# Moving the PEER score copies of token tiles 2 to 4 from VectorE to ScalarE in a diffusion backbone step

## The chip, the cores and the metric

The kernel runs on one core of one Trainium2 chip. The metric is the device time of one execution in microseconds. Three executions of the kernel before took 2545.37, 2546.10 and 2546.45 us, so the median is 2546.1 us.

## What is computed

One layer of a backbone with two token streams: 128 context tokens and 512 latent tokens, width 1024, all in f32. The tokens are cut into five tiles of 128: tile 0 is the context, tiles 1 to 4 are the latent. Each tile goes through adaLN, a gated linear recurrence, grouped-query attention, an output projection, and then through PEER, a product-key mixture of very many small experts:

```python
q = (xb @ w_q).reshape(n, P_HEADS, 2, P_QDIM // 2)
s = jnp.einsum('nhpd,hpkd->nhpk', q, sub_keys)        # 8 heads x 2 halves x 128 keys
s1, i1 = lax.top_k(s[:, :, 0], P_TOPK); s2, i2 = lax.top_k(s[:, :, 1], P_TOPK)
...                                                   # best 16 of the sums of pairs
u = jnp.take(w_u, idx, axis=0)                        # 16384 rows of 1024
act = gelu(jnp.einsum('nhkd,nd->nhk', u, xb))
v = jnp.take(w_v, idx, axis=0)
return jnp.einsum('nhk,nhkd->nd', g * act, v)
```

Every token reads 8 x 16 = 128 expert rows (u and v side by side, 8 KB).

## The kernel before

**Slots.** A slot is one expert of each of the 128 tokens of a tile: GpSimd (POOL) gathers 128 rows of 8 KB from HBM with an indirect DMA, VectorE takes the dot of the u half with the token (`dot_of`, line 1400), ScalarE applies Gelu and the routing weight (`w_slot`, lines 945 and 951), and the v half is added to an accumulator: by VectorE (`v_row`, line 1428), or by TensorE as a product with a diagonal matrix that ScalarE writes (line 961). A tile has 128 slots, five tiles have 640. VectorE also routes (lines 1320 to 1377: top 16, indices, softmax weights), 16 slots at a time.

**The plan.** Slots 0 to 191 are woven into the dense part of the layer. `plan_groups` writes down the order of all PSUM results (`NAMES`) and, by a cost of each result on TensorE (`STAGES`), the result behind which each slot stands (`SLOT_AT`). Every engine walks the same order; its `Beside` object runs the slots that are due before it turns to a result (`beside.before(name)`, inside `start` on TensorE and `group` on VectorE and ScalarE). For tile 1's first 64 slots (128 to 191) even slots are accumulated by `v_row`, odd slots by `v_odd` (line 570, matmuls at line 577), which TensorE does two slots later (`PE_LAG`). GpSimd gathers these slots one behind another (`gather_odd`, line 1223) into six buffers; one is free again when `v_row` or `v_odd` of its slot is done.

**Dense work around the change.** `post(b)` does the output projection, the second norm and the PEER scores for a batch of tiles; batch 2 is tiles 2, 3 and 4. Its last part is 16 rounds. In round m TensorE projects the queries (`qp`: 16 matmul records of 128x384) and, behind the next projection, multiplies them with the keys (`ss`: 6 matmul records of 128x128). Its order is qp 0, qp 1, ss 0, qp 2, ss 1, ... qp 15, ss 14, ss 15. ScalarE copies each qp result out of PSUM (line 1138), VectorE copies each ss result out in three pieces, one for each tile (line 1732). qp and ss results alternate over four PSUM banks, so that a qp has the bank of the qp before the last, and an ss that of the ss before the last.

**Behind the rounds.** The remaining 448 slots (64 of tile 1, 128 of each of tiles 2 to 4) run in loops without dense work. Their gathers go round eight buffers, three of them the ring that holds the weight slabs of the rounds, so GpSimd waits for the last ss result first (line 1280). VectorE reads the copied scores of tiles 2 to 4 only there. From tile 1's slot 192 on TensorE does all the accumulating (line 590). A tile ends with its gate and final norm (`tile_end`).

`step(...)` (lines 436 to 447) makes an engine wait for its own instruction before the next.

Of the kernel before, what the change touches and what calls it, by code (L numbers as in the profile page):

```python
# [32 lines left out]
ACT = mybir.ActivationFunctionType  # L33
AX = mybir.AxisListType.X

P = 128
# [10 lines left out]
PH, TOPK, NKEYS = 8, 16, 128  # L47
# [65 lines left out]
def turn_order(tiles):  # L113

    order = []
    for i in range(len(tiles) + 1):
        order.extend([("x2T", tiles[i])] if i < len(tiles) else [])
        order.extend([("h2", tiles[i - 1])] if i else [])
    return order
# [125 lines left out]
def build(nc, x_prompt, x_sample, cols, rows, normf_rows, brow, consts, masks, sel, cond_rows, ada_slabs, col_slabs, in_slabs, o_slabs,  # L245
          out_slabs, pq_slabs, uv, state, ckT, cv, y_prompt, y_sample, new_state, new_k, new_v):
    with ExitStack() as ctx:
# [3 lines left out]
        def sem(name):  # L251
            return ctx.enter_context(nc.semaphore(name))
# [108 lines left out]
        SC = [R1[:, 0:2048], HG[:, 2048:4096], R1[:, 0:2048], AB[:, 10240:12288], AB[:, 1024:3072]]  # L361
# [9 lines left out]
        def h_tile(t, k):  # L371
            return hTp[:, k, :] if t == 0 else hTl[:, k, (t - 1) * P:t * P]
# [44 lines left out]
        qkT_ready, sm_ready, p_ready, pT_ready, ob_ready = (sem("qkT_ready"), sem("sm_ready"), sem("p_ready"),  # L417
                                                            sem("pT_ready"), sem("ob_ready"))
        pn_ready, oT_ready, sig2_ready, m_ready = sem("pn_ready"), sem("oT_ready"), sem("sig2_ready"), sem("m_ready")
        h2T_ready, h2T_half, h2_ready, qp_ready = sem("h2T_ready"), sem("h2T_half"), sem("h2_ready"), sem("qp_ready")  # L420
        kv_out, state_out, y_out, nf_in, zb_ready = (sem("kv_out"), sem("state_out"), sem("y_out"), sem("nf_in"),
                                                     sem("zb_ready"))

# [49 lines left out]
        def wait_full(eng, name):  # L473

            banks, _, count = PLACE[name]
            eng.wait_ge(full[banks[0]], count)
            return psum(name)

        def freed(name):
            return [free[b] for b in PLACE[name][0]]  # L480
# [452 lines left out]
        def _(act):  # L933
            step = Steps(act, act_step)
            A = nc.scalar.activation
# [32 lines left out]
            def group(name):  # L968

                beside.before(name)  # L970
                return wait_full(act, name)
# [44 lines left out]
            for wc, dst, fn, ready in WT:  # L1016
                for m in range(4):
                    ps = group(("winP", wc, m))
# [90 lines left out]
            def tile_root(t):  # L1109
                act.wait_ge(fss_ready, t + 1)  # L1110
                A(st[:, 30:31], st[:, 29:30], ACT.Sqrt).then_inc(frt_ready, 1)

            def post(b):
                tiles, N = BATCHES[b], NB[b]
                lo, hi = tiles[0], tiles[-1] + 1
                beside.before(("x2T", lo))
                act.wait_ge(ssq_ready, NT + hi)
                step(A(st[:, 16 + lo:16 + hi], st[:, 8 + lo:8 + hi], ACT.Sqrt), *[rms_ready] * len(tiles))
                act.wait_ge(am_ready, 3)
                for name, t in turn_order(tiles):  # L1120
                    ps = group((name, t))
                    if name == "x2T":
                        for k in range(KD // 2):
                            step(A(h_tile(t, k), ps[:, k * P:(k + 1) * P], ACT.Identity,
                                   scale=AM[:, 1, min(t, 1), k:k + 1], bias=ADA[:, 2, min(t, 1), k:k + 1]))
                        act.sem_inc(freed((name, t))[0], 1)
                        act.sem_inc(h2T_ready, 1)
                    else:
                        if t == 0:
                            act.wait_ge(state_out, 32)  # L1130
                        step(A(H2[t], ps, ACT.Copy), *freed(("h2", t)), h2_ready)
                if b == 1:
                    tile_root(0)
                for m in range(2 * PH):
                    ps = group(("qp", b, m))
                    if m >= 2:
                        wait_full(act, ("ss", b, m - 2))
                    step(A(QP[b][:, m % 2, :], ps[:, 0:N], ACT.Copy), *freed(("qp", b, m)), qp_ready)
                    if b == 1 and m == 6:
                        expos(PH)  # L1140

# [11 lines left out]
            for wc, dst, fn, ready in WT:  # L1153
                for m in range(4):
                    ps = group(("winT", wc, m))
# [145 lines left out]
        def _(dve):  # L1301
            step = Steps(dve, dve_step)
# [131 lines left out]
            def group(name):  # L1434

                beside.before(name)
                return wait_full(dve, name)
# [59 lines left out]
            for n in range(NFIRST):  # L1497
                row(n + 1)
                s, q = ADA_SEGS[n // 4], n % 4
                ps = group(("mod", n))  # L1500
# [16 lines left out]
            for n in range(NFIRST + 1, NADA):  # L1517
                col_dots(next(cols))
                row(n)
                t = n - XT_FROM  # L1520
# [175 lines left out]
            def post(b):  # L1696
                tiles, N = BATCHES[b], NB[b]
                if b == 0:
                    dve.wait_ge(gate_ready, 8)
                else:  # L1700
                    dve.wait_ge(xr_in, 64)
                for q in range(4):
                    for t in tiles:
                        cs = slice(q * SC_W, (q + 1) * SC_W)
                        ps = group(("y", q, t))
                        gate = (G1P if t == 0 else G1L)[:, cs]
                        step(V.tensor_tensor(SQ2[b][:, 0:SC_W], ps[:, 0:SC_W], gate, ALU.mult), *freed(("y", q, t)))
                        step(V.tensor_tensor(X1[t][:, cs], X1[t][:, cs], SQ2[b][:, 0:SC_W], ALU.add))
                        if q == 3:
                            ssq(X1[t], t, SQ2[b])  # L1710
                beside.before(("x2T", tiles[0]))
                for t in tiles[:2]:
                    normed(NT + t, X1[t], xn2(t))
                for i, t in enumerate(tiles):
                    if i > 1:
                        beside.before(("x2T", t))
                        normed(NT + t, X1[t], xn2(t))
                    ps = group(("x2T", t))
                    for k in range(KD // 2, KD):
                        step(V.tensor_scalar(h_tile(t, k), ps[:, k * P:(k + 1) * P], AM[:, 1, min(t, 1), k:k + 1],  # L1720
                                             ADA[:, 2, min(t, 1), k:k + 1], ALU.mult, ALU.add))
                    dve.sem_inc(freed(("x2T", t))[1], 1)
                    dve.sem_inc(h2T_half, 1)
                if b == 1:
                    tile_end(0)
                    step(V.memset(PL[:, :], 0.0))
                    dve.sem_inc(v_done, NPE)
                for m in range(2 * PH):
                    ps = group(("ss", b, m))
                    ms = slice(m * NKEYS, (m + 1) * NKEYS)  # L1730
                    for i, t in enumerate(tiles):
                        step(V.tensor_copy(SC[t][:, ms], ps[:, i * P:(i + 1) * P]))
                    for x in freed(("ss", b, m)):
                        dve.sem_inc(x, 1)
                    if b == 1 and 1 <= m <= 6:
                        route(PH, 2 * m - 2, 2 * m)
                    if b == 1 and 7 <= m < 7 + EARLY // 2:
                        route(PH + 1, 2 * m - 14, 2 * m - 12)
# [54 lines left out]
            post(2)  # L1793
            beside.rest()
            dve.wait_ge(h2_ready, NT)
            for t in range(1, NT):
                def pass_(p, last):
                    for h in range(2):
                        j = t * PH + p * 2 + h
                        nxt = early = None  # L1800
                        if not last:
                            nxt = route_parts(j + 1, 1 - h, SC[t], 0)
                            early = route_parts(j + 2, h, SC[t], (p * 2 + h + 2) * 2 * NKEYS)
                        else:
                            if not h or t + 1 < NT:
                                nxt = route_parts(j + 1, 1 - h, SC[t], 0)
                            if t + 1 < NT:
                                early = route_parts(j + 2, h, SC[t + 1], h * 2 * NKEYS)
                        for k in range(TOPK):
                            i = h * TOPK + k  # L1810
                            dot(j * TOPK + k, k, h, GB_, gb_in,
                                16 * ((t * TSLOT - NSLOT) // NGB) + p * (16 * HSLOTS // NGB) + 16 * (i // NGB + 1), H2[t])
                            ahead = early if ROUTE_AT.get(k, EARLY) < EARLY else nxt
                            if k in ROUTE_AT and ahead:
                                ahead(ROUTE_AT[k])

                if t == 1:
                    pass_(2, False)
                else:
                    with dve.Fori(0, 3) as p:  # L1820
                        pass_(p, False)
                pass_(3, True)
                tile_end(t)
# [81 lines left out]
```

## Time and profile before

| what | value |
|---|---|
| median of the three runs | 2546.1 us |
| the profiled execution | 2541.14 us, of which its span is 2539.3 us |
| mean granted TensorE clock | 0.929 |
| busy: TensorE, VectorE, ScalarE, GpSimd | 79%, 69%, 37%, 37% |
| moved by DMA | 805.53 MB, 317 GB/s over the span |
| the 16 rounds of tiles 2 to 4 | about 1256 to 1383 us of the span |
| the loops behind them | from 1383.9 us to the end |

Busy time says how long an engine executed, not whether anybody waited for it; for that the timeline of each engine and the list of waits are read, stretch by stretch.

### The profile page before, as it was taken

How to read it: one execution, taken by the hardware profiler on the slowest of the kernel's cores; microseconds unless marked ns; L12 is line 12 of the kernel's file. 1: busy time of each engine (PE TensorE's matmuls, PEld its weight loads, DVE VectorE, ACT ScalarE, POOL GpSimd, SP SyncE). 2: the span in 40 equal slices, each digit the busy share in tenths (PEclk: the TensorE clock that was granted, in tenths of full speed). 3: DMA queues.
4: the chain of work that ended last, by engine and by line, in shares of the span. 5: the costliest groups of instructions: out<-in, count | busy, mean ns of one | idle time of the engine just before them, and what ended most of it. 6: DMA issues, size and time to landing. Idle time of an engine off the chain costs nothing. (4 is left out here: it accounts for less than half of the span.)

```text
span 2539.3 us, 27322 instructions
## 1 busy us (share of the span) xinstructions
PE 2006.7 (79%) x6925; PEld 1101.4 (43%) x6925; DVE 1748.4 (69%) x3969; ACT 945.2 (37%) x2456; POOL 938.2 (37%) x774
## 2 busy tenths in 40 slices
PE   6978897966677798778698776887778887687876
PEld 2667844755566543366454222322223222232222
DVE  2732277886776678767787777777777777777764
ACT  1402144223343434312332444444444444344443
POOL 0020022232222122202233554656545666456654
PEclk9998998987888899889899998999999999999999
DMA  8844677851111498859798999999999999999997
GB/s 318 291 150 170 227 297 294 328 209 67 67 67 67 159 339 328 325 217 402 271 367 323 422 421 393 419 422 422 421 400 412 422 422 421 410 406 422 422 421 327
DMA packets 113299, 805.53 MB, mean 317 GB/s; under 512 B 12596, under 2 KB 14006, under 8 KB 17046
## 3 DMA queue, kind: packets, MB, share of 16 engines
q0 software_dynamic: 93760, 680.96, 66.7%
q1 hardware_dynamic: 17704, 118.17, 12.6%
q10 hardware_dynamic: 1712, 4.98, 0.5%
q8 instruction: 50, 0.82, 0.1%
q14 instruction: 73, 0.60, 0.1%
HBM read 800.79 MB, written 3.28 MB: 317 GB/s over the span
## 5 line engine op out<-in xcount | busy, mean ns | idle before, releaser
L1201 POOL DMA_INDIRECT RG<-in_uv,idxs x264 | 351.2, 1330 | 568.0 <-DVE pl L1428 328.0
L945 ACT ACTIVATE agel<-apre 128x1 f32<-128x1 f32 x640 | 129.2, 202 | 990.3 <-DVE apre L1400 987.2
L590 PE MATMUL pl<-RG,BP 128*128 128x512 f32 x576 | 294.0, 636 | 106.7 <-ACT BP L961 106.0
L590 PE MATMUL pl<-RING,BP 128*128 128x512 f32 x576 | 282.2, 621 | 62.2 <-ACT BP L961 60.8
L615 PE MATMUL pa<-HL,RING 128*128 128x512 f32 (+2 forms) x960 | 315.5, 487 | 8.5 <-DVEq L447 8.1
L1400 DVE CUSTOM_DVE_ANT_0 R<-RG,AB 128x1024 f32<-128x1024 f32 x201 | 246.7, 1230 | 101.9 <-DMA RG<-in_uv,idxs 81.9
L1201 POOL DMA_INDIRECT RING<-in_uv,idxs x168 | 253.3, 1508 | 155.7 <-PE pl L590 68.6
L1400 DVE CUSTOM_DVE_ANT_0 R<-RING,AB 128x1024 f32<-128x1024 f32 x168 | 205.9, 1226 | 95.0 <-DMA RING<-in_uv,idxs 78.1
L615 PEld LDWEIGHTS pa<-HL,RING 128*128 128x128 f32 x960 | 166.3, 196 | 149.8 <-issue 119.1
L590 PEld LDWEIGHTS pl<-RG,BP 128*128 128x128 f32 x576 | 99.8, 192 | 294.0 <-ACT BP L961 220.1
L961 ACT ACTIVATE BP<-CT,wexp 128x128 f32<-128x128 f32 x480 | 192.7, 401 | 53.4 <-PE pl L590 15.9
L590 PEld LDWEIGHTS pl<-RING,BP 128*128 128x128 f32 x576 | 104.1, 194 | 235.6 <-ACT BP L961 145.6
L951 ACT ACTIVATE wexp<-agel,gws 128x1 f32<-128x1 f32 x640 | 188.7, 295 | 22.4 <-ACT agel L945 0.3
L1201 POOL DMA_INDIRECT EB<-in_uv,idxs x88 | 118.1, 1342 | 148.1 <-DVE pl L1428 95.5
L1428 DVE SCALAR_TENSOR_TENSOR pl<-RG,wexp,pl 128x1024 f32<-128x1024 f32 x118 | 151.6, 1285 | 7.5 <-ACT wexp L951 7.3
L1400 DVE CUSTOM_DVE_ANT_0 R<-RG,BP 128x1024 f32<-128x1024 f32 x96 | 117.7, 1226 | 52.3 <-DMA RG<-in_uv,idxs 29.0
L615 PE MATMUL pa<-RING,AB 128*128 128x256 f32 (+2 forms) x432 | 104.2, 392 | 30.6 <-DVEq L447 26.1
L615 PE MATMUL pa<-RING,HL 128*128 128x256 f32 x448 | 108.4, 405 | 24.9 <-ACTq L447 24.9
L1400 DVE CUSTOM_DVE_ANT_0 R<-EB,AB 128x1024 f32<-128x1024 f32 x67 | 82.4, 1230 | 59.8 <-DMA EB<-in_uv,idxs 58.6
L590 PE MATMUL pl<-HL,BP 128*128 128x512 f32 x192 | 94.8, 616 | 25.1 <-ACT BP L961 25.0
L945 ACT ACT_TABLE_LOAD x86 | 110.3, 1283 | 9.9 <-ACT RING L1084 2.8
L615 PEld LDWEIGHTS pa<-RING,HL 128*128 128x128 f32 x448 | 89.9, 204 | 43.8 <-ACTq L447 24.7
(277 smaller groups left out, 3133.8 us busy)
## 6 DMA issues: line engine op xcount, KB each, us to landing
RING<-in_in_slabs SPq DMA_DIRECT2D x42, 1024.0 KB, 5.2
RING<-in_pq_slabs SPq DMA_DIRECT2D x24, 1152.0 KB, 5.5
RING<-in_ada_slabs SPq DMA_DIRECT2D x16, 1024.0 KB, 5.2
RING<-in_out_slabs SPq DMA_DIRECT2D x12, 1024.0 KB, 5.6
RG<-in_col_slabs POOLq DMA_DIRECT2D x8, 1024.0 KB, 6.9
RING<-in_o_slabs SPq DMA_DIRECT2D x8, 1024.0 KB, 5.6
RG<-in_uv,idxs POOLq DMA_INDIRECT x297, 12.3
RING<-in_uv,idxs POOLq DMA_INDIRECT x168, 14.5
```

The lines of the kernel that those rows point to most:

```text
L590: last = nc.tensor.matmul(acc[:, c * 512:(c + 1) * 512], DG[:, k % 2, :], bufs[k % len(bufs)][:, D + c * 512:D + (c + 1) * 512], start=Fal ...
L615: return nc.tensor.matmul(out, l, r, start=s, stop=e)
L945: A(agel[:, par, k:k + 1], apre[:, par, k:k + 1], ACT.Gelu).then_inc(gel_done, 1)
L951: A(wexp[:, par, k:k + 1], agel[:, par, k:k + 1], ACT.Copy, scale=gws[:, par, k:k + 1]).then_inc(w_done, 1)
L961: A(DG[:, i % 2, :], ident, ACT.Copy, scale=wexp[:, par, k:k + 1]).then_inc(dg_done, 1)
L1201: nc.gpsimd.indirect_dma_start(out=bufs[b], out_offset=None, in_=uv, in_offset=bass.IndirectOffsetOnAxis(ap=idxs[:, par, k:k + 1], axis=0) ...
L1400: V.tensor_tensor_reduce(out=SCR[k % 2], in0=buf[:, 0:D], in1=hc, scale=1.0, scalar=0.0, op0=ALU.mult, op1=ALU.add, accum_out=apre[:, par, ...
L1428: V.scalar_tensor_tensor(PL[:, :], (GC[i % NGC] if t else GA[n % NGA])[:, D:2 * D], wexp[:, n // TOPK % 2, n % TOPK:n % TOPK + 1], PL[:, : ...
```

## The change

VectorE's `post` returns for batch 2 before its copies. ScalarE, having copied the queries qp m, runs the slots that are due before ss m-1, waits for ss m-1 and copies its three pieces into the same places; behind the last queries it also does ss 15. It releases the PSUM bank, and counts a new semaphore, on which VectorE waits once, after the slots of the plan and ahead of the loops.

```diff
@@ ScalarE, post(b)
                     step(A(QP[b][:, m % 2, :], ps[:, 0:N], ACT.Copy), *freed(("qp", b, m)), qp_ready)
+                    for i in ([m - 1] if m else []) + ([m] if m == 2 * PH - 1 else []):
+                        if b == 2:
+                            ps = group(("ss", b, i))
+                            for a, t in enumerate(tiles):
+                                step(A(SC[t][:, i * NKEYS:(i + 1) * NKEYS], ps[:, a * P:(a + 1) * P], ACT.Copy))
+                            for x in freed(("ss", b, i)) + [sc_ready]:
+                                act.sem_inc(x, 1)
@@ VectorE, post(b)
+                if b == 2:
+                    return
                 for m in range(2 * PH):
                     ps = group(("ss", b, m))
@@ VectorE, ahead of the loops
             dve.wait_ge(h2_ready, NT)
+            dve.wait_ge(sc_ready, 2 * PH)
```

## Rows read from the trace of the kernel before

**Rows 1.** The page: busy tenths in 40 slices of the span
```profile
PE   6978897966677798778698776887778887687876
DVE  2732277886776678767787777777777777777764
DMA  8844677851111498859798999999999999999997
```

**Rows 2.** Stretches: length, busy us of PE, PEld, DVE, ACT, POOL; PEclk, DMA share, GB/s
```profile
1256.00:1384.00 128.00, 127.54 (x432) 74.59 (x431) 107.81 (x249) 42.07 (x125) 36.47 (x36) 1.00 0.90 348
...
1376.00:1384.00 8.00, 7.75 (x31) 4.68 (x30) 7.50 (x17) 2.79 (x9) 0.14 (x1) 1.00 0.10 41
...
1392.00:1420.00 28.00, 23.05 (x44) 8.01 (x43) 21.09 (x51) 12.54 (x37) 14.11 (x12) 0.93 1.01 422
...
1384.00:1660.00 276.00, 208.86 (x432) 76.59 (x431) 199.32 (x481) 117.92 (x346) 150.20 (x110) 0.95 1.00 410
```

**Rows 3.** PE in order of time, the last rounds: start us, us, work [idle before]
```profile
1364.84 5.33 PE L615 MATMUL pa<-HL,RING 128*128 128x384 f32 x16
1370.00 1.88 PE L577 MATMUL po<-EB,BP 128*128 128x512 f32 x4
1371.72 0.83 PE L615 MATMUL pa<-RING,HG 128*128 128x128 f32 x6
1372.76 1.96 PE L577 MATMUL po<-BP 128*128 128x512 f32 x4 [0.21 <-ACT BP L961]
1374.55 5.32 PE L615 MATMUL pa<-HL,RING 128*128 128x384 f32 x16
...
1381.43 1.50 PE L615 MATMUL pa<-RING,HG 128*128 128x128 f32 x12
```

**Rows 4.** POOL in order of time, where the plan ends and the loops begin
```profile
1372.15 0.94 POOL L1223 DMA_INDIRECT EB<-in_uv,idxs  x1 [4.99 <-PE po L577]
1383.86 0.94 POOL L1201 DMA_INDIRECT RING<-in_uv,idxs  x1 [10.77 <-DVE pl L1428]
```

**Rows 5.** DMA queues from 1383 us to the end: packets, MB, share
```profile
q0 software_dynamic: 64512, 469.79, 98.1%
```

**Rows 6.** DVE groups, 1180 to 1410 us: busy us, mean ns | idle before
```profile
L1732 DVE COPY AB<-pa 128x128 f32<-128x128 f32 x32 | 9.3, 291 | 1.1
...
L1732 DVE COPY R<-pa 128x128 f32<-128x128 f32 x16 | 4.6, 289 | 0.8
```

**Rows 7.** ACT groups by form, whole span
```profile
L1138 ACT ACTIVATE HG<-pa 128x128 f32<-128x128 f32 x32 | 8.8, 274 | 43.5 <-PE pa L615 43.3 <-ACT HG L1138 0.2
...
L1138 ACT ACTIVATE HG<-pa 128x384 f32<-128x384 f32 x16 | 7.8, 489 | 36.4 <-PE pa L615 36.4
...
L1124 ACT ACTIVATE HL<-pa,ADA,AM 128x128 f32<-128x128 f32 x16 | 7.3, 455 | 8.7 <-PE pa L618 8.3
```

**Rows 8.** Who waited for whom, 1256 to 1384 us: us in total, times, longest
```profile
ACT agel L945 <- DVE apre L1400: 45.6, 27, 3.9
ACT HG L1138 <- PE pa L615: 36.4, 14, 5.5
...
PE po L577 <- ACT BP L961: 0.5, 2, 0.2
```

**Rows 9.** ACT in order of time: four of the 16 query copies, one wait
```profile
1324.04 0.47 ACT L1138 ACTIVATE HG<-pa 128x384 f32<-128x384 f32 x1
...
1355.11 0.49 ACT L1138 ACTIVATE HG<-pa 128x384 f32<-128x384 f32 x1
...
1362.66 0.49 ACT L1138 ACTIVATE HG<-pa 128x384 f32<-128x384 f32 x1 [0.25 <-PE pa L615]
...
1379.91 0.49 ACT L1138 ACTIVATE HG<-pa 128x384 f32<-128x384 f32 x1 [1.35 <-PE pa L615]
...
1390.61 0.20 ACT L945 ACTIVATE agel<-apre 128x1 f32<-128x1 f32 x1 [7.48 <-DVE apre L1400]
```

**Rows 10.** DVE in order of time, the end of the rounds
```profile
1383.24 0.28 DVE L1732 COPY R<-pa 128x128 f32<-128x128 f32 x1
...
1384.64 0.62 DVE L1732 COPY AB<-pa 128x128 f32<-128x128 f32 x2
1389.27 1.23 DVE L1400 CUSTOM_DVE_ANT_0 R<-RING,AB 128x1024 f32<-128x1024 f32 x1 [4.01 <-DMA RING<-in_uv,idxs]
```

More of the change, by code:

```diff
@@ L419, in build @@
         pn_ready, oT_ready, sig2_ready, m_ready = sem("pn_ready"), sem("oT_ready"), sem("sig2_ready"), sem("m_ready")
-        h2T_ready, h2T_half, h2_ready, qp_ready = sem("h2T_ready"), sem("h2T_half"), sem("h2_ready"), sem("qp_ready")
+        h2T_ready, h2T_half, h2_ready, qp_ready, sc_ready = sem("h2T_ready"), sem("h2T_half"), sem("h2_ready"), sem("qp_ready"), sem("sc_ready")
         kv_out, state_out, y_out, nf_in, zb_ready = (sem("kv_out"), sem("state_out"), sem("y_out"), sem("nf_in"),
```

## The prediction

> **What bounds the kernel now.** I read the slices of the span first. From the middle on, the DMA row shows nine tenths or more in every slice but the last [rows 1]: this is the part of pure slots. The stretches say how full: 422 GB/s from 1392 to 1420 us, and 410 GB/s, at a DMA share of 1.00, over 276 us with a tile's end in it [rows 2]. The queue of gathers moves 469.79 MB there [rows 5], which at 422 GB/s is 1113 us of the 1155 us that are left from 1383.9 us on. So the second half is bound by DMA, and all that a change ahead of it can do is to let it start earlier or later. It starts with the first gather of the loops, at 1383.86 us [rows 4].
>
> What sets that start? Not the gathers of the plan: the last of them went out at 1372.15 us, and then GpSimd waited for 10.77 us [rows 4]. The row blames VectorE's accumulation, but the code asks for the last score result there (line 1280), and TensorE was at it from 1381.43 to 1382.93 us [rows 3]; the accumulation that the row names merely ended near by, at about 1383.2 us, where the next VectorE copy starts [rows 10]. A wait for several things is put down to the last event, so I go by the code: **TensorE's last ss opens the loops.**
>
> And TensorE does not wait in the 16 rounds. Of the 128 us from 1256 to 1384 it is busy for 127.54 us, at a granted clock of 1.00 (2.4 GHz), against 107.81 us of VectorE and a DMA share of 0.90 [rows 2]. One round is a projection of 5.33 us, a pair of slot products of 1.88 us, and the scores of 0.83 us, end to end [rows 3]. In the whole list of waits of the stretch TensorE has two, of 0.5 us together, both for ScalarE's diagonals [rows 8]. ScalarE in turn waits for VectorE's dots (45.6 us in 27 pieces) and for the projections (36.4 us in 14) [rows 8]. VectorE's copies have no releaser on the list at all: it comes to every ss when this is long there, so it is late against TensorE, but nobody on the path minds.
>
> **The change, part by part.**
>
> *VectorE gives up 48 copies.* They are 32 of 291 ns and 16 of 289 ns, 13.9 us busy, and 1.9 us of gaps in front of them [rows 6]: 15.8 us off VectorE over the rounds, a bit less than 1 us each. What waits for VectorE in the rounds? ScalarE's slots, through them TensorE's odd products and GpSimd's buffers. But TensorE's products are placed in its order and it has no more idle time to give than the 0.21 us ahead of 1372.76 us and the 0.25 us or so behind the last ss [rows 3, 8]. The first is on the way to the last ss; a dot about 1 us sooner removes it: **-0.2 us**. The second lies behind the last ss and is hidden by the landing of the first gather. The rest turns into VectorE idle time: it will wait for gathers and for ScalarE's weights, where now it copies. GpSimd's even buffers may come free sooner; the odd ones follow TensorE as before.
>
> *ScalarE takes 48 copies.* Its own copy of this very shape out of PSUM took 274 ns (32 of them, the queries of the other batches) [rows 7]. That is 13.2 us busy. The nearest dearer row is the 128x128 with scale and bias from a table of columns, 455 ns [rows 7], which would make it 21.8 us; I take 274 ns, since it is the same operation on the same line, and 0.95 us for a group of three with its gaps, the rate of VectorE's. ScalarE's busy time in the stretch rises from 42.07 us [rows 2] to some 55 us of 128 (64 us by the upper price); it stays the idlest but GpSimd. Copy needs no table of its own: the copies at lines 951 and 961 already sit between Gelus.
> The Trainium skill, ScalarE: Activation LUTs, What ACT_TABLE_LOAD costs, gives an ACTIVATE with immediate scale and bias 186 ns + 0.833 ns an element, an estimate of 293 ns here; by it the 48 are 14.1 us, and the rest of the sum stands. The same page, Rules for kernel authors, speaks against the change: it gives plain operations to VectorE, which it calls up to about three times faster in bf16. For these f32 copies out of PSUM this trace does not agree: 274 ns on ScalarE, 289 to 291 on VectorE [rows 6, 7].
>
> *The new wait on ScalarE.* Behind the copy of qp m ScalarE runs the slots due there (mostly two), waits for ss m-1 and copies it. Queued behind that wait are a few slots and the copy of qp m+1. TensorE does ss m-1 directly behind qp m (with one slot pair between), and qp m+1 takes 5.33 us more, so ss m-1 is there when ScalarE has done its two slots, and the three copies fall into the time in which it now waits for the projection. In 13 of the 16 rounds that wait is over 0.95 us; in three it is 0, 0 and 0.25 us [rows 9]. In these the query copy could come up to 1 us later. Who waits for it? ss m, which stands behind the projection of m+1: qp 14 was copied before 1371 us, and qp 15 took until 1379.87 us before the pair with ss 14 [rows 3]. Cover of over 5 us, so **0**. The one short place is the end, where no projection stands between qp 15 and its scores: the copy ended at 1380.40 us and ss 15, the second half of the last 1.50 us, starts at about 1382.2 [rows 3, 9]. Cover 1.8 us there, with 1.35 us of idle ahead of the copy: **0**, and without the cover at most 0.95.
>
> *PSUM banks.* ss m+1 needs the bank that ScalarE now frees behind ss m-1, two rounds or about 15 us later: 0.
>
> *The wait of VectorE for all 16 groups.* Behind the last ss (1382.93 us) ScalarE has two groups to copy, done at about 1385.4 us counted from 1383.1, when its last diagonal of the plan was ready. VectorE now finishes its own copies at 1385.26 us and then idles until 1389.27 us for the gather; ScalarE idles 7.48 us until 1390.61 [rows 9, 10]. Cover 3.9 us: **0**. No DMA issue moves and SyncE's slab loads follow TensorE alone.
>
> **Sum.** -0.2 us. The profiled execution would go from 2541.14 to 2540.9 us. It lies 5.0 us under the median of the three runs, so one execution is no yardstick for the last 0.2%; against the median the forecast is 2545.9 us. About 0.2%, 5 us, is what a measurement of this kernel can tell from no change.
>
> **Rivals.**
>
> *VectorE is the real pacer* (faster). For it: 84% busy in the rounds, never waiting for an ss, and 45.6 us of ScalarE waits on it [rows 2, 8]. If the rounds could shrink by what it gives up, they would meet the DMA share first: 0.90 of 128 us is 115.2 us, so at most 12.8 us, giving 2533.3 us. This needs TensorE to have idle time that its modelled ends hide. Against it: 16 records of a projection in 5.33 us, 5.32 us in the next, at full clock, is the pace of an engine that is not fed late. The Trainium skill, Perfetto Trace Analysis, Optimizing Scalar/DVE Operations, names this case: where VectorE is saturated, moving work to ScalarE may pay. By that rule, the trace has VectorE near saturation but not on the path. Chance 0.09.
>
> *ScalarE becomes the pacer* (slower). If in each round the query copy and ss end up in series, because the slots behind which the copies stand are held by late dots, each of 15 rounds pays 0.95 us: 14.3 us, 2560.4 us. It decides when ScalarE comes to a query copy more than about 5 us after the projection's end; only then has TensorE an idle gap ahead of ss. For it: ScalarE walks its order strictly, and its waits for dots last up to 3.9 us. Against it: the dots come sooner than before, and the trace has three rounds without slack before the copy, none with a delay of TensorE. Chance 0.05.
>
> *The start of the loops moves, but not by ScalarE's queue:* VectorE has fewer, ScalarE more instructions to fetch, and both enter the loops at other moments. The loops are DMA-bound, so I give this a share of the rest and no direction: 0.03 beyond 5 us either way.
>
> **How the numbers follow.** Forecast 0.83, VectorE the pacer 0.09, ScalarE the pacer 0.05, the shift 0.03, half to each side. Faster by over 0.2%: 0.10; within: 0.83; slower: 0.07. The range holds the forecast's own spread: down to 2541.0 us, as the profiled execution lies 5 us under the median; up to 2550.5 us, for the three rounds without slack and the end each losing 0.95 us, 3.8 us, and about 0.8 us for the scatter of the runs. Both rivals at full price lie outside.
>
> **What would show it.** Right: TensorE still busy for all but about 0.3 us of the rounds; 48 ScalarE copies of about 275 ns; VectorE with about 14 us less busy time and more idle for gathers and weights; the first loop gather within 1 us of 1383.9; the same 422 GB/s after it. Wrong: TensorE gaps ahead of ss with ScalarE's query copy as the releaser, a first dot of the loops waiting for the copies, or rounds shorter than the 7.5 us that a projection, one slot pair and one ss take now [rows 3].

## The result: slower by 0.8%, and the profile after

Over eight executions each on one chip, the changed kernel took 2561.1 us (median; 2555.25 to 2573.0), the kernel before 2543.9 us (2530.35 to 2546.64). The ratio is 1.008, with a 95% interval of 1.0062 to 1.0099: **slower by 0.8%, about 20 us** (the two medians lie 17 us apart, the two profiled spans 20.8), where 2545.9 us and no measurable change were forecast. The profiled execution of the changed kernel took 2561.95 us, its span is 2560.1 us, and its mean granted TensorE clock is 0.927 against 0.929 before.

The page of the changed kernel: busy time of each engine, then the DMA's busy tenths and rates in 40 slices.

```profile
PE 2011.0 (79%) x6925; PEld 1105.6 (43%) x6925; DVE 1736.1 (68%) x3921; ACT 957.5 (37%) x2504; POOL 907.7 (35%) x774
DMA  8845677851121589859698999999999999999997
GB/s 322 291 145 176 234 294 302 316 185 66 66 82 55 204 318 343 329 216 402 258 376 330 421 421 378 422 422 422 421 402 421 418 396 412 379 419 405 390 421 306
```

The rates of the kernel before, from its page:

```profile
GB/s 318 291 150 170 227 297 294 328 209 67 67 67 67 159 339 328 325 217 402 271 367 323 422 421 393 419 422 422 421 400 412 422 422 421 410 406 422 422 421 327
```

The DMA tenths of the second half look the same as before [rows 1]. The rates don't: between about 2050 and 2430 us of the changed kernel there are slices of 396, 379, 405 and 390 GB/s, where the lowest before is 406.

First the 16 rounds. This is the changed kernel in the stretch of [rows 2], in that order of columns:

```profile
1256.00:1384.00 128.00, 128.00 (x435) 74.71 (x434) 96.58 (x204) 54.02 (x172) 38.31 (x36) 1.00 0.89 349
```

Its GpSimd timeline at the end of the rounds (start, duration, line, and in brackets the idle time before it with its releaser), which answers to [rows 4]:

```profile
1372.97 0.94 POOL L1230 DMA_INDIRECT EB<-in_uv,idxs  x1 [4.35 <-PE po L577]
1384.23 0.94 POOL L1208 DMA_INDIRECT RING<-in_uv,idxs  x1 [10.32 <-PE pa L615]
```

And the ScalarE groups of 1256 to 1400 us, by line and shape (count, busy us, mean ns, idle before):

```profile
L1143 ACT ACTIVATE AB<-pa 128x128 f32<-128x128 f32 x32 | 8.9, 278 | 1.0
...
L1138 ACT ACTIVATE HG<-pa 128x384 f32<-128x384 f32 x16 | 7.9, 491 | 44.1 <-PE pa L615 44.1
L1143 ACT ACTIVATE R<-pa 128x128 f32<-128x128 f32 x16 | 4.3, 268 | 1.8 <-issue 0.8 <-PE pa L615 0.6 <-ACT AB L1143 0.2
```

TensorE is busy for all of the 128 us, VectorE for 11.2 us less than before and ScalarE for 12.0 us more. The first gather of the loops goes out at 1384.23 us, 0.4 us later than before, and here its releaser is TensorE's score product, as the code said. The 20 us are not in the rounds. They lie behind them, in the 1150 us of loops that the change doesn't touch.

VectorE's longest waits in the loops (us in total, how often, the longest), first of the changed kernel, then of the kernel before:

```profile
DVE R L1407 <- DMA RING<-in_uv,idxs: 76.7, 80, 6.9
DVE R L1407 <- DMA RG<-in_uv,idxs: 75.8, 87, 2.2
DVE R L1407 <- DMA EB<-in_uv,idxs: 57.7, 50, 2.2
DVE R L1407 <- issue: 24.9, 19, 4.7
...
DVE BP L1329 <- issue: 6.1, 2, 3.1
```

```profile
DVE R L1400 <- DMA RG<-in_uv,idxs: 79.8, 94, 1.9
DVE R L1400 <- DMA RING<-in_uv,idxs: 78.1, 95, 4.0
DVE R L1400 <- DMA EB<-in_uv,idxs: 56.0, 51, 1.7
```

Time that waits for "issue", which is for nothing that the profile shows, has become 31.0 us on these two lines; before it is 2.9 and 1.2 us on the same two. VectorE's timeline of the changed kernel shows where (its pauses of over 3 us on slot work, all of them; the matching place of the kernel before follows):

```profile
1968.55 1.22 DVE L1407 CUSTOM_DVE_ANT_0 R<-RING,AB 128x1024 f32<-128x1024 f32 x1 [4.67 <-issue]
2053.01 1.23 DVE L1407 CUSTOM_DVE_ANT_0 R<-RING,AB 128x1024 f32<-128x1024 f32 x1 [4.63 <-issue]
2303.06 1.23 DVE L1407 CUSTOM_DVE_ANT_0 R<-RING,AB 128x1024 f32<-128x1024 f32 x1 [4.65 <-issue]
2307.93 0.09 DVE L1329 MATCH_VALUE_LOAD BP<-BP 128x8 f32 x1 [3.08 <-issue]
2387.45 1.23 DVE L1407 CUSTOM_DVE_ANT_0 R<-RING,AB 128x1024 f32<-128x1024 f32 x1 [4.63 <-issue]
2392.30 0.09 DVE L1329 MATCH_VALUE_LOAD BP<-BP 128x8 f32 x1 [3.05 <-issue]
```

```profile
1963.85 1.23 DVE L1400 CUSTOM_DVE_ANT_0 R<-RING,AB 128x1024 f32<-128x1024 f32 x1 [1.79 <-DMA RING<-in_uv,idxs]
```

The four of over 4.6 us stand ahead of the first dots of the second and third looped pass of tile 3, and of the same two of tile 4: the moments at which VectorE's hardware loop jumps back. In tile 4 a second pause of about 3.1 us follows 5 us later, at a routing instruction. Tile 2 has none. The DMA queues suggest what VectorE lacked: its instructions. From the start of the loops to the end, the changed kernel and then the kernel before:

```profile
q14 instruction: 50, 0.41, 0.1%
```

```profile
q14 instruction: 29, 0.24, 0.1%
```

There are 21 more fetches, of 8192 bytes each. The program of VectorE has lost 70 instructions ahead of its loops (4923 to 4853, counted in the built programs), and the loops themselves are the same. So the theory is: **the loops are the same, but they lie elsewhere.** Instructions come in pieces of 8192 bytes; if one takes 64 bytes, a piece holds 128 of them. A looped pass has 304 instructions on VectorE (counted in the trace from first dot to first dot) and touches three or four pieces, by its place. Touching three it stays loaded, touching four it is fetched again in every pass.

The length of each pass, worked out from the first dots in the timeline (us; the fourth pass of a tile holds the tile's end):

```
                 tile 2                 tile 3                 tile 4 (first three)
before           75.7 79.5 79.4 90.6    75.9 79.5 79.3 90.2    75.7 79.6 79.4
changed          75.7 79.5 79.3 90.6    79.5 84.5 81.1 89.4    79.6 84.4 81.0
```

Before rounding, tile 3 takes 334.4 us instead of 324.9, and tile 4's three passes 245.0 instead of 234.7: 9.5 and 10.3 us, together 19.8 of the 20.8 us between the two spans.

### The profile page after: what moved, and what is told of

It reads as the page before. It is cut to its first block and busy times, and to the rows that moved or that the text cites. A ratio compares the mean times of both kernels' runs of the same rounds, so it can differ in the third digit from the quotient of the medians.

```text
span 2560.1 us, 27332 instructions
## 1 busy us (share of the span) xinstructions
PE 2011.0 (79%) x6925; PEld 1105.6 (43%) x6925; DVE 1736.1 (68%) x3921; ACT 957.5 (37%) x2504; POOL 907.7 (35%) x774
## 5 line engine op out<-in xcount | busy, mean ns | idle before, releaser
L1208 POOL DMA_INDIRECT RG<-in_uv,idxs x264 | 341.9, 1295 | 558.0 <-DVE pl L1435 316.7
L590 PE MATMUL pl<-RING,BP 128*128 128x512 f32 x576 | 292.6, 643 | 81.2 <-ACT BP L961 79.6
L1208 POOL DMA_INDIRECT RING<-in_uv,idxs x168 | 235.3, 1401 | 214.0 <-PE pl L590 133.7
L1208 POOL DMA_INDIRECT EB<-in_uv,idxs x88 | 110.8, 1260 | 161.0 <-DVE pl L1435 100.5
```

The source lines that it names most:

```text
L590: last = nc.tensor.matmul(acc[:, c * 512:(c + 1) * 512], DG[:, k % 2, :], bufs[k % len(bufs)][:, D + c * 512:D + (c + 1) * 512], start=Fal ...
L1208: nc.gpsimd.indirect_dma_start(out=bufs[b], out_offset=None, in_=uv, in_offset=bass.IndirectOffsetOnAxis(ap=idxs[:, par, k:k + 1], axis=0) ...
```

## The experiments

All runs keep the whole computation. Ratios are against the kernel before on the same chip, with a 95% interval.

**1. Put the loops back where they were.** The change stays; 70 increments of a semaphore that nobody reads stand at the head of VectorE's program, over 1.3 ms ahead of the loops.

```diff
+            for _ in range(70):
+                dve.sem_inc(sem_pad, 1)
             dve.wait_ge(small_in, 64)
```

> The changed kernel with 70 semaphore increments that nobody waits for put at the head of VectorE's program, where it waits for its first inputs. The change took 70 instructions off VectorE's stream ahead of the loops (as the built program counts them); the filler puts every later VectorE instruction back where it stood in the kernel before, and nothing of the change is undone. Theory A (the loss is the place of VectorE's loops in its instruction stream: instructions are fetched in pieces of 8192 bytes, 128 instructions of 64 bytes, and a loop that touches four pieces is fetched anew in each pass): the 4.6 us issue gaps at the pass boundaries of tiles 3 and 4 go, the 8192-byte instruction fetches from 1384 us on fall from 50 to about 29, and the time is that of the kernel before, 2540 to 2548 us, ratio 0.998 to 1.002. Rival B (ScalarE's new copies or the new wait cost the time, through a later entry into the loops or a worse rhythm of the gathers): no change against the changed kernel, 2555 to 2565 us, ratio 1.008.

Measured: 2543.4 us, ratio 0.9997 (0.9983 to 1.0012). The rounds and the fetches from the start of the loops on:

```profile
1256.00:1384.00 128.00, 127.96 (x433) 74.38 (x431) 95.44 (x204) 54.24 (x173) 39.83 (x36) 1.00 0.89 348
```

```profile
q14 instruction: 30, 0.25, 0.1%
```

With the full change in the rounds and the loops in their old places nothing is lost, and nothing is won.

**2 to 5. Only move the loops of the kernel before,** with N = 58, 38, 78 and 128 of the same increments. 58 is 128 - 70, the place that the change gives them.

> The kernel before, with 58 such increments at the head of VectorE's program: 58 and minus 70 are the same place modulo 128, so its loops lie to the pieces of 128 as those of the changed kernel do, without any of the change. Theory A: about 2560 us, ratio 1.006 to 1.010, gaps of 4.6 us at the pass boundaries of tiles 3 and 4 but not of tile 2, some 50 instruction fetches of 8192 bytes in the loops. Rival B: no difference from the kernel before, ratio 1.000.

> The kernel before with 38 increments. By my count of the instructions each tile's loop starts 20 places further on in its piece of 128 than the one before it, and a loop of some 304 instructions touches four pieces when it starts beyond place 80. Theory A: only the loop of tile 4 lies badly: two gaps of 4.6 us instead of four, about half the loss, ratio 1.003 to 1.006. Rival B: ratio 1.000.

> The kernel before with 78 increments. Theory A: the loops of tiles 2 and 3 lie badly, and that of tile 4 as well if it still starts short of the next piece: two to three loops with gaps, ratio 1.008 to 1.014. Rival B: ratio 1.000.

> The kernel before with 128 increments at the head of VectorE's program, a whole piece of 8192 bytes. If what counts is the place within a piece of 128 instructions, the time is that of the kernel before: ratio 0.998 to 1.002, no gap of 4.6 us in the loops. If the filler itself costs something, or the loss grows with the amount moved, it is slower than the kernel with 78 increments: ratio 1.008 or more.

| moved by | time, us | ratio (95%) | tiles with the 4.6 us pauses | fetches in the loops |
|---|---|---|---|---|
| 38 | 2553.37 | 1.0053 (1.0028 to 1.0077) | 4 | 39 |
| 58 | 2561.72 | 1.0067 (1.0046 to 1.0089) | 3, 4 | 49 |
| 78 | 2563.32 | 1.0073 (1.0048 to 1.0097) | 2, 3 | 49 |
| 128 | 2542.43 | 0.9989 (0.9975 to 1.0004) | none | 29 |

VectorE's timeline with 58 and then with 78 instructions more (pauses of over 4 us):

```profile
1969.54 1.23 DVE L1402 CUSTOM_DVE_ANT_0 R<-RING,AB 128x1024 f32<-128x1024 f32 x1 [4.71 <-issue]
2053.91 1.23 DVE L1402 CUSTOM_DVE_ANT_0 R<-RING,AB 128x1024 f32<-128x1024 f32 x1 [4.62 <-issue]
...
2304.23 1.22 DVE L1402 CUSTOM_DVE_ANT_0 R<-RING,AB 128x1024 f32<-128x1024 f32 x1 [4.63 <-issue]
...
2389.26 1.23 DVE L1402 CUSTOM_DVE_ANT_0 R<-RING,AB 128x1024 f32<-128x1024 f32 x1 [4.66 <-issue]
```

```profile
1642.72 1.23 DVE L1402 CUSTOM_DVE_ANT_0 R<-RING,AB 128x1024 f32<-128x1024 f32 x1 [4.68 <-issue]
1727.48 1.22 DVE L1402 CUSTOM_DVE_ANT_0 R<-RING,AB 128x1024 f32<-128x1024 f32 x1 [4.62 <-issue]
1978.69 1.22 DVE L1402 CUSTOM_DVE_ANT_0 R<-RING,AB 128x1024 f32<-128x1024 f32 x1 [4.64 <-issue]
...
2063.45 1.22 DVE L1402 CUSTOM_DVE_ANT_0 R<-RING,AB 128x1024 f32<-128x1024 f32 x1 [4.65 <-issue]
```

The kernel before, moved by 58, becomes the changed kernel: the same tiles, the same pauses, the same time, and not one copy moved. 128 more instructions cost nothing and change nothing: the places repeat after 128, which with fetches of 8192 bytes makes 64 bytes an instruction. The ratios lie within what was expected, but for the one moved by 78, which at 1.0073 is a little under its 1.008. The rule of three or four pieces also gives which tiles: the loops of tiles 2, 3 and 4 begin 20 places apart (304 instructions of a loop and 228 behind it are 532, four times 128 and 20 more). If that of tile 2 begins at place x of its piece, 304 instructions stay within three pieces up to place 80. Moved by 38 only tile 4 is beyond (x + 78), by 58 tiles 3 and 4 (x + 78, x + 98), by 78 tiles 2 and 3 (x + 78, x + 98), while tile 4 has come round to the next piece (x + 118). With x between 10 and 22 all of these hold; x itself was fitted to these runs and not read from the program.

**6. Is ScalarE really covered?** As 1, and every score copy on ScalarE is done twice.

```diff
-                            step(A(SC[t]..., ps[...], ACT.Copy))
+                            for _ in range(2):
+                                step(A(SC[t]..., ps[...], ACT.Copy))
```

> The changed kernel with VectorE's loops put back in their place (70 increments) and each of ScalarE's 48 score copies done twice. If the prediction was right that the copies lie in ScalarE's waiting time (cover over 5 us a round against 0.95 us a group), 1.9 us a group is hidden too: ratio 0.998 to 1.002, TensorE busy for over 127 of the 128 us from 1256 us on. If ScalarE is near the path, each round loses up to 0.95 us: up to 14 us, ratio 1.005.

Measured: 2544.95 us, ratio 1.0005 (0.9988 to 1.0022). Its ScalarE groups of 1256 to 1400 us:

```profile
L1146 ACT ACTIVATE AB<-pa 128x128 f32<-128x128 f32 x64 | 17.7, 277 | 2.0
...
L1140 ACT ACTIVATE HG<-pa 128x384 f32<-128x384 f32 x16 | 7.8, 489 | 34.2 <-PE pa L617 33.7 <-ACT AB L1146 0.5
```

96 copies instead of 48 cost nothing that can be measured; ScalarE's idle time ahead of the query copies falls from 44.1 to 34.2 us, which is where they go. The rival of ScalarE as the pacer is out.

**7 to 9. Is a pause of VectorE enough?** The pauses could be only a sign. So the kernel before gets pure VectorE pauses at the head of each of the nine looped passes: two products of 128x2048 (2.29 us each, 4.7 us with their waits) in 7, three (about 7 us) in 9, and in 8 the two with two of about 1 us more ahead of slots 18 and 31 of a pass. 8 and 9 have 119 increments as well, to put the loops in a good place.

```diff
                     with dve.Fori(0, 3) as p:
+                        for i in range(2):
+                            V.tensor_tensor(HG[:, 0:2 * D].rearrange("p (a b) -> p a b", a=2), G2[:], G2[:],
+                                            ALU.mult).then_inc(sem_pause, 1)
+                            dve.wait_ge(sem_pause, (t - 2) * 6 + p * 2 + i + 1)
                         pass_(p, False)
```

> The kernel before with two VectorE products of 128x2048 f32 (the gates with themselves, into a dead buffer), about 4.7 us together, at the head of each of the 9 loop passes of tiles 2 to 4; the loops stay in a good place. The changed kernel had four gaps of 4.6 us and two of 3.1 us more than the kernel before and lost about 18 us. If a pause of VectorE at a pass head goes to the end in full, because the eight gather buffers have no slack over their round trip, 9 pauses cost about 42 us: ratio 1.014 to 1.018. If the buffers absorb part, less than half of that; and then the fetches of the changed kernel must cost in another way than through VectorE's gaps.

> What is open: two products of 4.7 us at the head of every pass cost 15 us in all, only in the first pass of each tile, while the badly placed loops lose 5 us in each repeated pass. This kernel is the kernel before with the same head pause and two more VectorE products of about 1 us in a pass, ahead of its slots 18 and 31, where the dots of the changed kernel came 1 us late as well; it stays in a good place (119 increments at the head). Reading 1 (the pauses of VectorE are all there is, and past some 5 us a pass the slack is used up): the repeated passes take 82 to 85 us instead of 79.5, in all 9 passes, ratio 1.010 to 1.016. Reading 2 (the fetches do harm besides VectorE's pauses): the repeated passes stay at 79.5 to 80.5 us, ratio 1.006 to 1.008.

> The kernel before with three such products, about 7 us, at the head of each pass. Reading 1: 2 us or more a pass go beyond the slack, repeated passes of 81.5 to 83 us, ratio 1.011 to 1.016. Reading 2: the slack of a pass is larger than 7 us, repeated passes of 79.5 us, and only the first pass of a tile pays: ratio 1.008 to 1.009 (21 us).

Measured: 7 took 2557.1 us (ratio 1.0059, 1.0038 to 1.0081), 8 took 2566.05 us (1.0093, 1.0071 to 1.0114), 9 took 2567.61 us (1.0098, 1.0077 to 1.012). The passes of tile 3:

```
before                      75.9 79.5 79.3 90.2
7, pause of 4.7 us          79.4 80.0 75.8 94.4
9, pause of 7 us            80.7 79.6 73.5 97.5
changed, fetching 4.6 us    79.5 84.5 81.1 89.4
```

Nine pauses of 4.7 us cost 15 us, about 5 us a tile, not 42: the first of a tile shows, the next ones are taken up (a second pass of 80.0 us), since eight buffers of rows have landed meanwhile. Fetching pauses only twice a tile and costs 10. In 8 the added pauses moved tile 4's loop into a bad place (85.0 and 84.2 us there), by a misjudged margin, so that its ratio decides nothing, and 8 tells only of tiles 2 and 3, whose second passes stayed at 79.5 us. 9 lies between its two readings: the second pass is 79.6 us in tile 3, but 81.3 in tile 2 and 80.7 in tile 4. By the sums of the rows above tile 3 loses 4.7 us in 7, 6.4 in 9 and 9.6 in the changed kernel. **A pause explains about half of the price,** and some six tenths if run 9's 6.4 us are held against tile 4's 10.3, whose two pauses come to 7.7 us; the rest must come from something else that the fetches do. (The granted clock of 7 to 9 is a little lower, 0.914 to 0.924 against about 0.93; whether that adds to their time wasn't tried, and it would make the share of the pause smaller.)

**10. Fetch without a pause.** SyncE has nothing to do in the loops. Here it runs 600 increments in each looped pass, over four pieces, and has to fetch them; VectorE's program is that of the kernel before.

```diff
             for t in range(1, NT):
+                if t > 1:
+                    with sp.Fori(0, 3) as p:
+                        sp.wait_ge(v_done, t * TSLOT + V0 + p * 32)
+                        for _ in range(600):
+                            sp.sem_inc(sem_sp, 1)
                 sp.wait_ge(y_ready, t + 1)
```

> The kernel before, with SyncE (idle in the loops) executing 600 semaphore increments at the start of each of the 9 looped passes of tiles 2 to 4. At 64 bytes each that is more than four fetches of 8192 bytes a pass, some 40 to 50 more fetches in all, while VectorE's own program and its places stay. It asks whether the fetches cost DMA time by themselves, without any engine on the path waiting for them. Theory 'late DMA engine': each fetch lengthens the queue of one of the 16 DMA engines, a gather is complete only with its slowest engine, so dots that wait for data start 2 to 5 us behind the time at which, by count, that many gathers had landed (0.6 us in the kernel before, 3 to 5 us in the badly placed loops); VectorE never pauses, so eight buffers still cover it, and the time rises by 0 to 5 us: 2544 to 2549 us. Rival 'the pause is all': the delay of dots stays at 0.6 us and the time does not move: 2543.5 to 2544.5 us.

**11. Both:** SyncE's fetches of 10 and VectorE's pauses of 7.

> The same SyncE fetches together with the pure VectorE pause of 4.7 us at the head of each looped pass (the pause alone gave 2557.1 us, with passes of 79.1, 79.5 and 75.8 us in tile 2). It asks why a pause by fetching costs about 10 us a tile and the same pause without fetching 5. Theory 'late DMA engine': fetches and pause together eat the lead of the eight buffers, the DMA runs dry behind a pass boundary as in the changed kernel, the second looped pass of a tile grows from 79.5 to about 84 us, and the time is some 10 to 15 us above the pause alone: 2565 to 2572 us. Rival 'the pause is all' (what differs is where VectorE is stopped, not the DMA): 2557 us, passes as with the pause alone.

Measured: 10 took 2570.8 us, ratio 1.0123 (1.0099 to 1.0147); 11 took 2582.19 us, ratio 1.0173 (1.0149 to 1.0197). Both lie above every range that was expected. The instruction fetches of run 10 from the start of the loops on, and its longest waits of VectorE there:

```profile
q14 instruction: 83, 0.68, 0.1%
```

```profile
DVE R L1407 <- DMA RG<-in_uv,idxs: 94.2, 102, 1.9
DVE R L1407 <- DMA RING<-in_uv,idxs: 91.2, 101, 4.1
DVE R L1407 <- DMA EB<-in_uv,idxs: 60.2, 52, 2.0
...
DVE R L1407 <- issue: 2.0, 1, 2.0
```

VectorE is held for "issue" no more than before (2.0 us against 2.9 on this line), and still 54 more fetches cost 29.5 us, far more than the 0 to 5 us expected: 0.55 us for 8 KB whose packet takes 0.31 to 0.34 us in the loops of these traces, and that at 422 GB/s would be 0.02 us. VectorE waits for gathered rows instead, 245.6 us in these three groups against 213.9 before. Fetches (1.23%) and pauses (0.59%) together give 1.73%: they nearly add up. The second looped passes of 11 take 84.7, 84.4 and 84.5 us, as its theory said.

**Why a fetch is so dear** is seen where the gathers run out, at the end. The stretches of 1 us of the kernel before (last gather issued at 2510.79 us) and of the changed kernel (at 2531.62 us); the last two columns are the DMA share and GB/s:

```profile
2522.00:2523.00 1.00, 0.50 (x2) 0.11 (x1) 0.00 (x0) 0.78 (x3) 0.00 (x0) 1.00 0.47 197
2523.00:2524.00 1.00, 1.00 (x3) 0.52 (x4) 0.91 (x1) 0.00 (x0) 0.00 (x0) 1.00 0.20 82
2524.00:2525.00 1.00, 0.88 (x3) 0.05 (x1) 0.32 (x2) 0.58 (x3) 0.00 (x0) 1.00 0.06 25
```

```profile
2539.00:2540.00 1.00, 1.00 (x3) 0.45 (x3) 1.00 (x1) 0.00 (x0) 0.00 (x0) 1.00 0.77 320
2540.00:2541.00 1.00, 0.76 (x2) 0.00 (x0) 0.21 (x2) 0.69 (x3) 0.00 (x0) 1.00 0.16 66
2541.00:2542.00 1.00, 0.74 (x2) 0.49 (x3) 0.56 (x1) 0.21 (x1) 0.00 (x0) 1.00 0.06 25
2542.00:2543.00 1.00, 1.00 (x3) 0.19 (x1) 0.68 (x2) 0.26 (x2) 0.00 (x0) 1.00 0.06 25
```

A share of 0.06 is one engine of 16. Before, the engines finish within some 3 us. In the changed kernel nearly all are done shortly after 2540 us, and from 2541 us on the share is that of about one engine for over 4 us. The last dot waits for it: it starts at 2546.37 us. A gather is complete only with its slowest engine. In the middle of the loops the same can be counted from the DMA records, in which a gather ends with 16 completions: how long after the 16 x n-th completion of the loops does their n-th dot start, where it waits for data? With all engines level that is short; with one behind it grows by what this one is late. Medians of the second and third looped passes, us:

```
                                   tile 2       tile 3       tile 4
before                             1.4 1.5      0.6 0.6      0.6 0.6
changed                            0.7 0.7      4.5 5.6      2.9 2.7
2, before moved by 58              0.7 0.7      4.9 5.5      3.0 3.2
7, pauses of 4.7 us alone          0.7 0.7      0.7 0.7      0.7 0.7
9, pauses of 7 us alone            0.7 0.7      0.6 0.6      0.6 0.6
10, SyncE's fetches alone          4.8 6.1      3.7 5.3      5.9 6.5
```

The delay is there where there are fetches, whichever engine makes them, and pauses alone don't bring it. In run 10 one can see it grow: at 1648 us it is 2.2 us, after the fetch at 1649.73 us 2.9, and it stays so for three dots while SyncE goes on with its increments; after the fetch at 1657.59 us it is 3.6, and further fetches take it to 6.8. So it is the fetches of that run and not its 5400 increments that set an engine back. Of 26 fetches of run 10 that stand alone between two dots waiting for data, 18 raised the delay by 0.55 us or more (mostly 0.6 to 0.8) and 8 not at all; between 97 pairs of such dots without a fetch the median change is 0.0. That is the 0.55 us of a fetch found above: **a fetch sets one DMA engine back by some 0.65 us, and as every gather needs that engine, the whole stretch pays it.**

The lead of eight buffers shrinks by the delay. When VectorE then pauses, the other engines run out of rows. In the changed kernel, behind the pause that ended at 2053.01 us:

```profile
2050.00:2055.00 5.00, 1.49 (x4) 0.38 (x2) 1.69 (x6) 1.33 (x4) 0.94 (x1) 0.89 1.02 421
2055.00:2060.00 5.00, 4.62 (x6) 2.04 (x7) 3.97 (x12) 1.78 (x7) 0.03 (x1) 0.50 0.84 347
2060.00:2065.00 5.00, 5.00 (x12) 1.90 (x10) 4.67 (x7) 1.86 (x7) 3.09 (x3) 0.92 0.65 234
```

GpSimd (POOL, the fifth busy time) waits 6.7 us for TensorE to free a buffer (its next gathers go out at 2052.30 and 2059.97 us), and the DMA falls to 347 and 234 GB/s. Run 7 at the same pass boundary, behind a pause of the same length:

```profile
2050.00:2055.00 5.00, 3.48 (x6) 1.26 (x7) 4.08 (x16) 1.80 (x6) 0.10 (x1) 0.78 1.02 423
2055.00:2060.00 5.00, 4.98 (x11) 2.03 (x10) 4.64 (x10) 1.80 (x6) 2.72 (x3) 0.88 1.01 421
```

GpSimd stands still there too, for 5.2 us, but with no engine late the DMA has enough queued and stays at 421 GB/s. TensorE's granted clock goes down after its idle time in both (0.50, which is 1.2 GHz, and 0.78 as means of 5 us).

## Why the prediction was wrong

- **The rounds: right.** TensorE idle for about 0.3 us of them was forecast, 0.0 came; 48 ScalarE copies of about 275 ns, they took 278 and 268; about 14 us off VectorE, 11.2 less busy in the stretch; the first gather within 1 us of 1383.9, it went out at 1384.23. The -0.2 us can't be seen. (The 7.5 us of a round in its last sign is a slip: 5.33, 1.88 and 0.83 us make 8.0. Nothing rests on it.) Of its signs of being right only "the same 422 GB/s after it" failed.
- **ScalarE's cover: right,** and wider than claimed (run 6 takes it twice).
- **VectorE is no pacer: right.** 11 us off it won nothing (run 1: 0.9997).
- **The sum: wrong, for a term it doesn't have.** The step that failed is in the third rival: "VectorE has fewer, ScalarE more instructions to fetch, and both enter the loops at other moments. The loops are DMA-bound, so I give this a share of the rest and no direction: 0.03 beyond 5 us either way." It named the instructions, but took their number and the moment for what matters, not the place of the loops, and took being DMA-bound for a cover. It is the reverse: because the loops are DMA-bound, what an instruction fetch does to one DMA engine is paid in full (run 10: 29.5 us for 54 fetches), and the changed kernel pays 20 us for 21 more fetches and VectorE's waits for them. The row of instruction fetches stood in the profile (q14, 29 of them in the loops, hardly any in the repeated passes of a tile), and its price was never bounded. At the prices that these runs show, which the record before them did not have, its term would have been: two loops of three that cross into a fourth piece, at 10 us each, +20 us.
- **Its range and chances** followed from that: +4.6 us at the top, and 0.07 for slower. That the rival of ScalarE as the pacer gave 2560.4 us, near the result, is chance; its mechanism didn't occur.
- How the 10 us of a tile divide is an estimate: the pause about 5 us by run 7, ten more fetches at the 0.55 us of run 10 another 5.5.

What stays open: why a fetch sets its DMA engine back by some 0.65 us where its own packet takes 0.31 to 0.34, and which engine serves it, as the records don't name the engine; that some fetches raise the delay and others don't would fit different engines, but isn't shown. Whether ScalarE's own 80 instructions more cost anything wasn't tried apart; run 1 leaves no room for more than 0.12%.

## What to carry to other kernels

Ahead of a hardware loop about as long as this one (304 instructions), a change of the instruction count moves the loop against the fetched pieces; count the instruction fetches within the loop before and after, and look for idle time put down to "issue" at the first instruction of a pass. Where an edit far ahead changes the time of an untouched loop, shift the loop by increments that do nothing: 128 of them cost nothing here (0.9989), and one run tells place from substance. This loop, bound by DMA, didn't hide its instruction fetches, as a gather waits for the engine that they delay.

## What the runs showed of the hardware that was not expected

- VectorE's instructions come in fetches of 8192 bytes, and the effect of a loop's place repeats after 128 instructions (run 5). A loop of about 304 was kept when it touched three such pieces and fetched again in every pass when it touched four, at a pause of 4.6 to 4.7 us and 10 us in all a tile.
- 54 fetches by an engine that nobody waits for cost a DMA-bound stretch 29.5 us (run 10), 0.55 us each; most of those that can be seen alone there set one DMA engine back by 0.6 to 0.8 us.
- At a rate of 421 to 423 GB/s one of the 16 DMA engines was 4 us and more late (changed kernel, 2040 to 2055 us), and a gather over all of them is as late as that engine. The mean DMA share doesn't show it; the stretches at the end, where the share falls to 0.06 for several us, do.
